# Router tiles in their own buffers, two down weights loaded earlier, and ScalarE copying both result halves of the last two expert passes

## What is computed

```python
x = x + hybrid_mixer(rmsnorm(x, g0), ...)      # forgetting attention (8 heads of 64), a recurrence, a convolution
x = x + cross_attention(rmsnorm(x, g1), mem_n, w_xq, w_xkv, w_xo)
x = x + hierarchical_moe(rmsnorm(x, g2), ...)  # 4 groups of 4 experts, 2 of one group's 4 for each token
return rmsnorm(x, final_norm_g)

# forgetting attention: logits s[t,s] = q_t.k_s * scale + (c_t - c_s), causal, softmax, times v
# experts: g = argmax of the group logits; top 2 experts of that group by softmax of the router logits
#   hid = silu(t @ w_gate[e]) * (t @ w_up[e]);  out += combine * (hid @ w_down[e])
```

## Time and profile before

| what | value |
|---|---|
| time, median of 3 runs | 720.63 us (720.16 to 722.01) |
| the profiled execution's own time | 721.87 us |
| its span from first to last instruction | 720.1 us |
| PE busy in the span | 683.2 us (95%) |
| DVE, ACT, POOL busy | 281.8, 152.1 and 76.8 us |
| bytes moved by DMA | 111.91 MB, mean 155 GB/s |
| granted TensorE clock, mean | 0.992 |

### The profile page before, as it was taken

How to read it: one execution, slowest core, us unless ns; L and a number is a source line. 1 busy time by engine, 2 the same in 40 slices (tenths; PEclk the granted TensorE clock), 3 DMA queues, 4 the chain that set the end, 5 groups by cost and what they waited for, 6 DMA issues and landing times.

```text
span 720.1 us, 8431 instructions
## 1 busy us (share of the span) xinstructions
PE 683.2 (95%) x3398; PEld 333.3 (46%) x3398; DVE 281.8 (39%) x673; ACT 152.1 (21%) x313; POOL 76.8 (11%) x106
## 2 busy tenths in 40 slices
PE   6999999999989899999999999999999999998993
PEld 4744444453547565444444446545564333332331
DVE  3207599927144564303120006413335712212156
ACT  3010351003282444211000003302111110101012
POOL 2000081502020000000000000000001110100052
PEclk9999999999999999999999999999999999999997
DMA  8903240303035513300019403030139999999773
GB/s 255 333 0 117 76 158 1 118 2 117 24 124 151 176 60 117 117 1 0 1 32 395 157 0 117 2 144 29 51 96 351 380 374 383 383 377 382 263 230 121
DMA packets 69941, 111.91 MB, mean 155 GB/s; under 512 B 5649, under 2 KB 43781, under 8 KB 69901
## 3 DMA queue, kind: packets, MB, share of 16 engines
q1 hardware_dynamic: 65724, 96.16, 38.8%
q0 software_dynamic: 4176, 15.21, 5.7%
HBM read 101.90 MB, written 9.46 MB: 155 GB/s over the span
## 4 chain that ended last, share of the span: by engine, by line
PE 80%; DMA 7%; SPq 4%; DVE 3%; ACT 3%; issue 1%; POOL 1%; DVEq 0%; POOLq 0%; ACTq 0%
PE bank L1904 26%; PE bank L2180 15%; PE bank L1780 8%; PE bank L1914 6%; PE bank L1806 3%; DMA W<-in_w_up_dram 2%; PE bank L2250 2%; PE bank L1950 2%; PE bank L2230 2%; DMA n_sb<-y_dram,A 2%; PE bank L1936 2%; PE bank L2133 1%; DMA x_sb<-in_x_dram 1%; SPq L480 1%; PE bank L2111 1%
## 5 line engine op out<-in xcount | busy, mean ns | idle before, releaser
L1904 PE MATMUL bank<-hT,W 128*128 128x512 f32 x368 | 159.7, 593 | 0.9 <-DVE hT L1063 0.9
L2180 PE MATMUL bank<-W,n_sb 128*128 128x512 f32 x256 | 114.2, 596 | 0.7 <-ACT n_sb L1031 0.7
L1904 PEld LDWEIGHTS bank<-hT,W 128*128 128x128 f32 x368 | 69.4, 190 | 87.5 <-issue 86.0
L1780 PE MATMUL bank<-W,A 128*32 128x512 f32 x672 | 84.8, 594 | 5.5 <-issue 2.4
L2180 PEld LDWEIGHTS bank<-W,n_sb 128*128 128x128 f32 x256 | 47.1, 190 | 53.9 <-issue 52.3
L1413 DVE SCALAR_TENSOR_TENSOR A<-A,pc 128x511 f32<-128x511 f32 (+29 forms) x60 | 51.6, 860 | 2.0
L1780 PEld LDWEIGHTS bank<-W,A 128*32 128x32 f32 x672 | 23.9, 110 | 52.9 <-issue 50.9
L695 POOL TENSOR_TENSOR rstd<-ss,mhalf 128x1 f32<-128x1 f32 x14 | 7.7, 549 | 372.8 <-DVE ss L1047 208.3
L1806 PE MATMUL bank<-Dn,A 128*32 128x512 f32 x264 | 36.3, 595 | 0.0
L1262 DVE TENSOR_TENSOR A<-A,bank 128x256 f32<-128x256 f32 x12 | 5.1, 421 | 75.8 <-ACT A L825 75.8
L898 ACT ACTIVATE A<-bank 128x512 f32<-128x512 f32 (+1 forms) x22 | 12.1, 556 | 103.7 <-PE bank L1904 77.0
(11 more groups left out here) (306 smaller groups left out, 806.8 us busy)
## 6 DMA issues: line engine op xcount, KB each, us to landing
W<-in_w_gate_dram SPq DMA_DIRECT2D x14, 1024.0 KB, 14.5
W<-in_w_up_dram SPq DMA_DIRECT2D x14, 1024.0 KB, 15.1
Dn<-in_w_down_dram SPq DMA_DIRECT2D x11, 1024.0 KB, 13.6
W<-in_w_in_dram SPq DMA_DIRECT2D x5, 2048.0 KB, 9.2
W<-in_w_xkv_dram SPq DMA_DIRECT2D x4, 2048.0 KB, 8.2
hT<-in_w_down_dram SPq DMA_DIRECT2D x5, 1024.0 KB, 12.9
y_dram<-A POOLq DMA_DIRECT2D x10, 512.0 KB, 7.0
W<-in_w_out_dram SPq DMA_DIRECT2D x2, 2048.0 KB, 7.8
```

The source lines that it names most:

```text
L1780: mm = nc.tensor.matmul(PS[2 + b][r, :], xgT[:, b, c, r], gu_at[GU_HOME[e]][:, c, :], start=c == 0, stop=c == DC - 1)
L1904: mm = nc.tensor.matmul(bank[0:w, 0:n], lhs, src[:, c, 0:n], start=c == 0, stop=c == DC - 1)
L2180: mm = nc.tensor.matmul(PS[k % 4][:, :], src[:, c, t * P:(t + 1) * P], W[:, (n_load + n) % SLOTS, c, :], start=first and j == 0, stop=last ...
```

## The change

The router gets two buffers of its own in `A` (`routeT`, one for even and one for odd token tiles; the second takes the place that `fgain` has later). `hT` is therefore no longer used from the end of cross attention's input projection on, and the two down loads into it are issued right after the second expert's gate and up weights, without the wait for logits and rows. The load of `fgain` is issued after all weight refills. ScalarE copies both halves of passes 10 and 11 (`y_other_half`), and TensorE's waits go by ScalarE's count there. Two small VectorE instructions that prepare positions for overflow are moved into the overflow's branch. In forgetting attention the masks of the next pair are made one iteration later and at its end, behind `f_scale`. The diff, cut to its core:

```diff
+        routeT = [A[:, 4096:5120].rearrange("p (c t) -> p c t", c=DC), A[:, 7680:8704].rearrange("p (c t) -> p c t", c=DC)]
@@ experts_loads @@
                 load_gate_up(sp, TAKEN[k])
+            for e in TAKEN[:DN_HOMES]:
+                if DN_HOME[e] >= SLOTS:
+                    load_down(sp, e)
 
             sp.wait_ge(xo_ps, 2 * XH)
             for e in TAKEN[:DN_HOMES]:
                 if DN_HOME[e] in (0, 2):
                     load_down(sp, e)
-            sp.dma_start(fgain, final_norm_g...).then_inc(router_in, 16)
...
             load_gate_up(sp, TAKEN[4])
-            sp.wait_ge(logits_ps, ST)
-            sp.wait_ge(xg_in[1], 16)
-            for e in TAKEN[:DN_HOMES]:
-                if DN_HOME[e] >= SLOTS:
-                    load_down(sp, e)
...
+            sp.wait_ge(logits_ps, ST)
+            sp.dma_start(fgain, final_norm_g...).then_inc(router_in, 16)
             sp.wait_ge(over_done, 1)
@@ ScalarE @@
+            def y_other_half(p):
+                act.wait_ge(y_ps, 2 * p + 2)
+                act.wait_ge(y_stored[p % 2], 16 * (p // 2))
+                nc.scalar.activation(ysb[:, p % 2, 512:1024], PS[6][:, :], ACT.Copy).then_inc(y_act, 1)
+
             for p in range(NP):
                 silu(p)
                 if p:
                     y_half(p - 1)
                 turned_hid(p)
+                if p - 1 >= NP - LATE:
+                    y_other_half(p - 1)
             y_half(NP - 1)
+            y_other_half(NP - 1)
@@ VectorE @@
+            def route_evac(t, k):
+                dve.wait_ge(turned, TURN0[3] + 2 * t + k + 1)
+                nc.vector.tensor_tensor(routeT[t % 2][:, 4 * k:4 * k + 4, :], PS[4 + k]..., gains..., ALU.mult).then_inc(turn_sb, 1)
...
-                    turn_evac(dve, 3, t - 1, 1, PS[5], hT, R_FFN)
+                    route_evac(t - 1, 1)
...
-                if p:
+                if p == 0:
+                    combine()
+                elif p - 1 < NP - LATE:
                     y_half(p - 1)
-                else:
-                    combine()
...
-            link(nc.vector.scalar_tensor_tensor(out=posm, in0=picked, scalar=-4096.0, in1=pos, op0=ALU.mult, op1=ALU.add))
-            link(nc.vector.tensor_scalar(posm, posm, 4096.0 - CAP + P, None, ALU.add))
             with dve.If(dve.value_load(over[0:1, 0:1]) > 0):
-                y_half(NP - 1)
+                link(nc.vector.scalar_tensor_tensor(out=posm, ...))
+                link(nc.vector.tensor_scalar(posm, posm, 4096.0 - CAP + P, None, ALU.add))
...
                     add_row(1, t, w2nd)
-                    if t == 0:
-                        y_half(NP - 1)
@@ forgetting attention, VectorE @@
-                if u % ST == 1 and u < UNITS - ST:
-                    f_mask(u // ST + 1)
                 if TURN_LAG <= u < UNITS + TURN_LAG:
                     f_pt(u - TURN_LAG)
                 if u < UNITS:
                     for a in range(2):
                         f_scale(u, a)
+                if u % ST == 2 and u < UNITS - ST:
+                    f_mask(u // ST + 1)
@@ TensorE @@
-                    mm = nc.tensor.matmul(PS[6][...], hT[:, c, t * P:(t + 1) * P], wgr[:, c, :],
+                    mm = nc.tensor.matmul(PS[6][...], routeT[t % 2][:, c, :], wgr[:, c, :],
...
                 for n, left in enumerate((y_act, y_dve)):
-                    if p:
+                    if p == NP - 1:
+                        pe.wait_ge(y_act, p + n)
+                    elif p:
                         pe.wait_ge(left, p)
...
                         if l == LATE - 1:
-                            pe.wait_ge(y_act, NP)
-                            pe.wait_ge(y_dve, NP)
+                            pe.wait_ge(y_act, NP + LATE)
```

More of the change, by code:

```diff
@@ L534, in experts_loads @@
                     load_down(sp, e)
-            sp.dma_start(fgain, final_norm_g.rearrange("(o d) -> o d", o=1).to_broadcast([P, D])).then_inc(router_in, 16)
             def store_rows(t):
@@ L564, in experts_loads @@
                         load_down(sp, e)
+            sp.wait_ge(logits_ps, ST)
+            sp.dma_start(fgain, final_norm_g.rearrange("(o d) -> o d", o=1).to_broadcast([P, D])).then_inc(router_in, 16)
             sp.wait_ge(over_done, 1)
@@ L1104, in full_mean @@
                 nc.vector.tensor_scalar(ss[:, n:n + 1], ss[:, n:n + 1], half_ss[:, t:t + 1], 1.0 / D, ALU.add, ALU.mult).then_inc(ms_done, 1)
+            gains = pc[:, R_FFN:R_FFN + DC]
+            def route_evac(t, k):
+                dve.wait_ge(turned, TURN0[3] + 2 * t + k + 1)
+                nc.vector.tensor_tensor(routeT[t % 2][:, 4 * k:4 * k + 4, :], PS[4 + k][:, :].rearrange("p (c t) -> p c t", c=4),
+                                        gains[:, 4 * k:4 * k + 4].rearrange("p (c o) -> p c o", o=1).to_broadcast([P, 4, P]),
+                                        ALU.mult).then_inc(turn_sb, 1)
             def choose(t):
@@ L1136, in place @@
                                             ALU.mult, ALU.mult).then_inc(pick_done, 1)
-            gains = pc[:, R_FFN:R_FFN + DC]
             def turned_rows(p):
@@ L1162, in experts_dve @@
                 add_half(t, 0)
-                turn_evac(dve, 3, t, 0, PS[4], hT, R_FFN)
+                route_evac(t, 0)
                 if t:
@@ L1167, in experts_dve @@
                 add_half(t, 1)
-            turn_evac(dve, 3, ST - 1, 1, PS[5], hT, R_FFN)
+            route_evac(ST - 1, 1)
             full_mean(ST - 1)
@@ L1289, in add_row @@
                                                in1=x_sb[:, t, :], op0=ALU.mult, op1=ALU.add).then_inc(fin_sum, 1)
-            link(nc.vector.scalar_tensor_tensor(out=posm, in0=picked, scalar=-4096.0, in1=pos, op0=ALU.mult, op1=ALU.add))
-            link(nc.vector.tensor_scalar(posm, posm, 4096.0 - CAP + P, None, ALU.add))
             with dve.If(dve.value_load(over[0:1, 0:1]) > 0):
-                y_half(NP - 1)
+                link(nc.vector.scalar_tensor_tensor(out=posm, in0=picked, scalar=-4096.0, in1=pos, op0=ALU.mult, op1=ALU.add))
+                link(nc.vector.tensor_scalar(posm, posm, 4096.0 - CAP + P, None, ALU.add))
                 dve.wait_ge(gu_ps, NP)
@@ L1679, in logits_half @@
                 for c in range(4 * k, 4 * k + 4):
-                    mm = nc.tensor.matmul(PS[6][:, t * (NG + EX):(t + 1) * (NG + EX)], hT[:, c, t * P:(t + 1) * P], wgr[:, c, :],
+                    mm = nc.tensor.matmul(PS[6][:, t * (NG + EX):(t + 1) * (NG + EX)], routeT[t % 2][:, c, :], wgr[:, c, :],
                                           start=c == 0, stop=c == DC - 1)
```

## The result

The changed kernel takes **712.93 us** (median of 5 runs, 712.21 to 714.75), the kernel before 720.63 (median of 5 runs of the same session, 717.93 to 722.01): ratio 0.989, 95% interval 0.9866 to 0.9914. The forecast was 714.7 with a range from 713.4.

What follows compares the result with a forecast made beforehand. The prediction took full DMA engines from 544 us and a busy PE as close limits, with PE's waits delaying the end in full. Gains of 1.94 + 3.97 = 5.91 us from 720.63 gave 714.7 us, range 713.4 to 717.6.

Steps and rivals of the forecast that it cites:

- Masks: Forgetting attention: the copy needs only the transposes, so unit 3's product no longer waits behind the masks; 1.94 us gained.
- 0.6 or more of cover: Forgetting attention: VectorE's idle time before the next scores covers the moved masks (1.29 us) with 0.6 us or more to spare.
- Early downs: Expert passes: two down loads issued early bring later weights sooner, removing PE's waits before passes 9 and 10; 3.97 us.
- The lead: Expert weights: how much earlier they land after the early down loads; bounds 5.4 and 7.0 us, the lower taken.
- The margin at pass 10: Expert passes: pass 10's weight, the next to be late, lands 1.4 to 3 us before it would delay PE.
- rival A: Expert weights: the lead is only half used because the queue runs empty; 717.2 us if 1.5 arrives; chance 0.12.
- The gain: End of SP's queue: the final gain's load lands at some 674, or under 682, before its use at 698.6; 0 us.
- rival C: Final sums: the gain lands last, at 705.0, and VectorE waits; 721.2 us; chance 0.06 together with another rival.
- the turns that the DMA engines take between queues: DMA engines: alternating packet by packet between queues with work, so GpSimd's gathers could not hold back the gain; cost 0.
- Router's buffers and copies: Router: same copies and products, 0 us; passes 10 and 11: ScalarE's copies gain 0 to 0.3 us, taken as 0.
- The sum: Whole kernel: 1.94 + 3.97 = 5.91 us gained, subtracted from the median 720.63 to give 714.7 us.

Runs made afterwards that it cites:

- the copies' run: Only ScalarE's copies of both result halves of passes 10 and 11 and the overflow's two moved instructions, against the kernel before: 722.07 us, ratio 0.9995.
- the two of before: Two profiled executions of the kernel before, nothing changed: 721.87 us in the first; the second sample's run measured 721.55 us, ratio 0.9987.
- the masks': Only forgetting attention's masks moved behind the scaling, one iteration later, against the kernel before: 719.96 us, ratio 0.9966.
- the downs': Only the router's own buffers, the two early down loads and the late load of the final gain, against the kernel before: 716.9 us, ratio 0.9926.
- the idle time put back: Changed kernel with three ScalarE copies into unused memory, TensorE waiting for the third before pass 10's product: 717.6 us, ratio 0.9932 to the kernel before.
- the second series: The changed kernel measured again without an edit, in a later session, against the kernel before: 714.45 us, ratio 0.9901.

## Why the forecast was right about the waits and too small in its size

**Masks.** 1.94 forecast, 1.98 measured in the profile with that edit alone and 1.99 with all. The reason given held: the copy starts with the transposes, at 242.68 while the scores run, and `pv` follows them. VectorE still stood 1.24 us before unit 7's scores, behind the masks that took 1.28 (0.6 or more of cover was forecast).

**Early downs.** 3.97 forecast, 4.11 measured. The lead can be read: pass 10's weight landed at 667.66 before and 657.3 after, 10.4 earlier, of which 3.20 and 1.99 come from ahead of the expert stage; that leaves 5.2, against the 5.4 taken. The margin at pass 10 became 1.1 us (1.4 to 3 forecast). So rival A, which decides under 3.97 us of lead, was 1.2 us away.

**The gain.** Landed at 670.5, 25 us before it is used (a bound of 674 to 682 was forecast); rival C never came near. It had landed before the first gather of the final chain was issued, so the turns that the DMA engines take between queues, on which the forecast rested rival C's end, were not tested here.

**Router's buffers and copies.** 0 forecast; the copies' run is 0.9995 of its base. ScalarE ended its last copy at 686.0, 0.7 us after the down product. TensorE needs it for its first spread product with rows of pass 11. By 14.00 us for 16 products that one is due at about 686.2 (an estimate from that row), so the copy was just in time, and the products show no idle time.

**The sum, and the step that failed.** Direct gain 6.1 against 5.91. The failing step is the last: "The median of the runs is 1.24 below the profiled one, so the forecast is 720.63 - 5.91". It prices each wait at its length, puts the clock behind the waits at nothing, and takes the profiled execution for a picture of them all. Of the five profiles of this program that keep a long idle time at the masks or at pass 10 (the two of before, the masks', the downs' and the copies'), with eight such places, six have half the clock behind the idle time, at 1.70 us a place; the two without are both in the one profile that the forecast was made from. The means say the same, less sharply. In the one session with clocks of both kernels, the lost clock was 6.14 us before and 4.75 after, 1.4 less; with the direct 6.1 that is 7.5, and the means differ by 7.3. Over all runs that list a clock it is 6.5 (74 runs) and 4.4 (11 runs), 2.1 less, and the means differ by 8.3 (721.77 and 713.50); but these 74 lack the base runs of the result's session, which were the fastest, and the 11 hold five from it. Compared at about the same mean clock the direct part is nearly alone. The table is rough, because the clock's fall in the tail is in the mean clock too:

| mean granted clock of a run | before: runs, mean us | changed: runs, mean us | difference |
|---|---|---|---|
| 0.995 to 0.997 | 3, 718.63 | 4, 712.39 | 6.2 |
| 0.993 to 0.994 | 19, 720.25 | 5, 713.94 | 6.3 |
| 0.991 to 0.992 | 28, 721.66 | 2, 714.62 | 7.0 |
| 0.987 to 0.990 | 24, 723.50 | none | |

The gain thus has two parts: 6.1 us of waits, and one to two more on average because the falls of the clock behind the two idle times no longer occur. The first rests on the segments of the profiles, the second on the six rows with half the clock and on the run that filled the idle times; its size is known only that roughly. The forecast left the clock out because the one profile showed it full behind both waits: 7.07 us for pass 10's product in the earlier trace rows, as for pass 11's. By the Trainium skill, "TensorE: Matmul & The Clock Gate", section "What's actually happening", the gate watches the engine's activity in a window that is free-running and does not start over with the kernel, so the same kernel can meet it differently from run to run. The nine places above, six with and three without a fall of the clock (the ninth is the idle time put back), are compatible with it. No run here shows the window itself. What stays open is what in an execution decides it, behind the same idle time; the place at 215 us does it in seven of twelve profiles with two idle times of 1.2 and 1.0 us close together, while 1.08 us alone at pass 10 did not, nor did the 1.08 to 1.53 us before pass 9 in four profiles.

**The range.** Its lower end was 1.3 below the forecast, from the spread of the copies and the profiled run alone. With the clock as a term (0 to 2 x 1.7), it would have reached to 711.3, and with one to two of it on average its centre would have been near 713. The miss itself is narrow and partly a matter of which executions were drawn: 712.93 lies 0.5 below the range, and the second series' 714.45 lies inside it. What the forecast had wrong is the missing term, not that half microsecond.

## What to carry to other kernels

Price an idle time of TensorE of some two microseconds at its length and, on average over executions, about one more for the clock that falls behind it; look at the granted clock in several executions before deciding that it doesn't. Before a gain is read from two profiles, take out the segments ahead of the change: here 3.2 of 9.8 us came from there. And if a wait can't be removed, products that nobody reads, run in its time, gave back 2 us of it here (0.7 to 3.5 by the interval). And compare a variant with the base of its own session: here the bases differed by up to 2 us, as much as the effects in question.

## What the runs showed of the hardware

- Behind idle times of TensorE of 1.9 to 2.8 us the granted clock fell to half in six of nine profiled cases, 1.70 us lost each time, and never where the idle time was gone or filled. Behind 1.08 to 1.53 us before passes 9 and 10 it stayed full in all five profiles that have such a wait. Of two kernels measured in one session, the one with 2.40 us of idle time put in lost 1.4 us more of clock on average than the one with 1.08 us, though its profile shows none behind that idle time.
- The same program, on the same data, spreads over 7.4 us (717.9 to 725.3 in 74 runs of the kernel before), and most of that goes with the mean granted clock (0.987 to 0.996; the correlation of time with lost clock is 0.88).
- With five gathers outstanding instead of three, ScalarE stood for 3.83 us with no operand outstanding in the profiled execution, and the kernel took 3.3 us more than the changed kernel in the same session. With four the profiles have no such stall.
- A wait that the profile puts down to "issue" at pass 10 was a DMA wait: as soon as other work stood before it, the profile named the weight's transfer.
